# A hybrid decoder layer in float32: in the FFN-in units the form T2 is made by an accumulating DMA instead of a VectorE sum

## What is computed

```python
def swiglu_ffn(x, w_in, w_out):
    gate, up = jnp.split(x @ w_in, 2, axis=-1)      # w_in: 2048 x 11008
    return (jax.nn.silu(gate) * up) @ w_out

x = x + 0.5 * swiglu_ffn(rmsnorm(x, ffn1_norm), ffn1_w_in, ffn1_w_out)
...
x = x + mixed @ w_out
x = x + 0.5 * swiglu_ffn(rmsnorm(x, ffn2_norm), ffn2_w_in, ffn2_w_out)
```

## Time and profile before

| | |
|---|---|
| median of 3 runs | 1762.74 us |
| profiled execution: its time | 1762.94 us |
| profiled execution: its span | 1760.9 us |
| TensorE busy | 1753.6 us |
| VectorE busy | 1451.9 us |
| ScalarE busy | 1077.2 us |
| DMA: moved, mean rate | 371.29 MB, 211 GB/s |
| granted TensorE clock | 1.00 in every stretch looked at (2.4 GHz) |

### The profile page before, as it was taken

One profiled execution on the slowest core, in us unless ns is written; L12 is line 12 of the kernel. 1 busy time (PEld: TensorE's weight loads), 2 busy tenths in 40 slices (PEclk: granted clock), 3 DMA queues, 4 the chain that ended last, 5 costly groups with the idle time before them and its releaser, 6 DMA issues.

```text
span 1760.9 us, 20876 instructions
## 1 busy us (share of the span) xinstructions
PE 1753.6 (100%) x8036; PEld 1462.5 (83%) x8036; DVE 1451.9 (82%) x1607; ACT 1077.2 (61%) x1359; POOL 53.9 (3%) x54
## 2 busy tenths in 40 slices
PE   9999999999999999999999999999999999999999
PEld 7888888888988888888888888888888888988887
DVE  7988888888899998575655655888888888899998
ACT  7666666666666666454545544666666666666665
POOL 0000000000000001100000000000000000000000
PEclk9999999999999999999999999999999999999999
DMA  9877666676655556555455447576777776664762
GB/s 378 256 238 236 221 215 215 215 225 190 225 215 190 204 215 209 181 189 181 156 189 165 170 168 263 145 233 219 226 236 236 237 236 216 207 207 164 259 215 88
DMA packets 165490, 371.29 MB, mean 211 GB/s; under 512 B 6184, under 2 KB 15936, under 8 KB 165264
## 3 DMA queue, kind: packets, MB, share of 16 engines
q1 hardware_dynamic: 152288, 342.02, 54.9%
q0 software_dynamic: 11984, 25.98, 7.9%
q10 hardware_dynamic: 1120, 1.97, 0.3%
HBM read 367.82 MB, written 3.69 MB: 211 GB/s over the span
## 4 chain that ended last, share of the span: by engine, by line
PE 95%; DVE 2%; SPq 1%; DMA 1%; issue 0%; ACT 0%; ACTq 0%; DVEq 0%
PE bank L582 9%; PE bank L580 9%; PE bank L581 9%; PE bank L564 7%; PE bank L566 7%; PE bank L565 7%; PE bank L521 7%; PE bank L523 7%; PE bank L522 7%; PE bank L651 5%; PE bank L652 5%; PE bank L653 5%; PE bank L678 3%; PE bank L677 3%; PE bank L679 3%; PE bank L549 1%
## 5 line engine op out<-in xcount | busy, mean ns | idle before, releaser
L1185 DVE TENSOR_TENSOR wlo<-raw,whi 128x1024 fp32r<-128x1024 f32 (+1 forms) x586 | 698.3, 1207 | 215.4 <-ACT whi L847 207.7
L847 ACT ACTIVATE whi<-raw 128x1024 fp32r<-128x1024 f32 (+1 forms) x586 | 611.2, 1047 | 379.6 <-PE bank L523 189.3
L580 PE MATMUL bank<-whi,xs 128*128 128x512 f32 (+1 forms) x768 | 297.6, 388 | 1.7 <-DVE xs L1374 1.6
L582 PE MATMUL bank<-whi,xs 128*128 128x512 f32 (+1 forms) x768 | 295.5, 385 | 0.0
L581 PE MATMUL bank<-wlo,xs 128*128 128x512 f32 (+1 forms) x768 | 295.3, 385 | 0.0
L847 ACT ACTIVATE whi<-tsum 128x1024 fp32r<-128x1024 f32 (+1 forms) x120 | 122.4, 1037 | 110.4 <-PE bank L582 64.1
L580 PEld LDWEIGHTS bank<-whi,xs 128*128 128x128 f32 x768 | 144.2, 188 | 30.1 <-DVE wlo L1371 2.2
L582 PEld LDWEIGHTS bank<-whi,xs 128*128 128x128 f32 x768 | 144.1, 188 | 27.7
L581 PEld LDWEIGHTS bank<-wlo,xs 128*128 128x128 f32 x768 | 144.3, 188 | 26.8
L651 PE MATMUL bank<-whi,aw_hi 128*128 128x512 f32 x420 | 164.0, 390 | 0.0
L653 PE MATMUL bank<-whi,aw_lo 128*128 128x512 f32 x420 | 163.5, 389 | 0.0
(11 more groups left out here) (204 smaller groups left out, 2704.7 us busy)
## 6 DMA issues: line engine op xcount, KB each, us to landing
raw<-ffn_w_in SPq DMA_DIRECT2D x158, 1024.0 KB, 7.1
raw<-ffn_w_out SPq DMA_DIRECT2D x84, 1024.0 KB, 6.5
raw<-w_in SPq DMA_DIRECT2D x48, 1024.0 KB, 5.0
tsum<-ffn_w_in POOLq DMA_DIRECT2D x18, 1024.0 KB, 8.5
raw<-w_out SPq DMA_DIRECT2D x16, 1024.0 KB, 4.9
raw<-ffn_w_in SPq DMA_DIRECT2D x16, 768.0 KB, 5.5
x<-x SPq DMA_DIRECT2D x4, 512.0 KB, 12.4
raw<-ffn_w_out SPq DMA_DIRECT2D x4, 512.0 KB, 3.6
```

Of the source, the lines that this page charges most:

```text
L580: mm(banks[b][:, 0:w], xs[:, k + i, 0, tok], hi, start=starts[b] and k + i == 0, stop=False, skip_group_check=True)
L582: last = mm(banks[b][:, 0:w], xs[:, k + i, 1, tok], hi, start=False, stop=k + i == last_k, skip_group_check=True)
L847: A(whi[:, h % SLOTS, 0:n_el], src, ACT.Copy).then_inc(weights_hi, 1)
L1185: V.tensor_tensor(wlo[:, h % SLOTS, 0:n_el], src, whi[:, h % SLOTS, 0:n_el].bitcast(f32), ALU.subtract).then_inc(weights_lo, 1)
```

## The change

T2 is made like T4: when both halves of T1 are split, a DMA of the POOL queue adds B22 from device memory onto T1 in `tsum` (`add_piece(u, j, "B22", T1, t2_added)`). `sum_t2` is gone; VectorE keeps T1 and T3. ScalarE waits for `t2_added` before it copies T2, and for the sum of T3 before it copies T3. `free` now names B11's split as the last reader of B11's raw buffer. B22 is thus read from device memory twice, once by SP's queue into its raw buffer and once by POOL's onto `tsum`.

```diff
--- before.py
+++ after.py
@@ -321,8 +321,8 @@
         ga_hi, ga_ready, gs_summed, gs_hi, gs_ready, out_sums, p1_copied, p_joined = (
             sem(n) for n in ("ga_hi", "ga_ready", "gs_summed", "gs_hi", "gs_ready", "out_sums", "p1_copied", "p_joined"))
         xg_ready, s_summed, s_hi, s_ready = (sem(n) for n in ("xg_ready", "s_summed", "s_hi", "s_ready"))
-        sums_done, t4_added, copied, w_done, gate_added, c11_done = (
-            sem(n) for n in ("sums_done", "t4_added", "copied", "w_done", "gate_added", "c11_done"))
+        sums_done, t2_added, t4_added, copied, w_done, gate_added, c11_done = (
+            sem(n) for n in ("sums_done", "t2_added", "t4_added", "copied", "w_done", "gate_added", "c11_done"))
         sq_done, hss_ready, hms_ready, hr_ready, hsc_ready, qn_ready, qk_psum, qkT_ready, v_ready = (
             sem(n) for n in ("sq_done", "hss_ready", "hms_ready", "hr_ready", "hsc_ready", "qn_ready", "qk_psum", "qkT_ready", "v_ready"))
         f_psum, f_copied, f_added, f_z_ready, f_m_ready, f_exped, f_logged, nlf_ready = (
@@ -347,9 +347,7 @@
                         j, i = (n - IN_P[u]) // 8, (n - IN_P[u]) % 8
                         if j == 0:
                             return weights_lo, IN[u] + 2 * i + 2
-                        if i == LOAD["B11"]:
-                            return sums_done, 3 * ((UNITS - 1) * u + j)
-                        last = {LOAD["B21"]: B21, LOAD["B12"]: T3, LOAD["B22"]: B22, LOAD["G0"]: G0, LOAD["G1"]: G1, LOAD["U0"]: U0, LOAD["U1"]: U1}[i]
+                        last = {LOAD["B11"]: B11, LOAD["B21"]: B21, LOAD["B12"]: T3, LOAD["B22"]: B22, LOAD["G0"]: G0, LOAD["G1"]: G1, LOAD["U0"]: U0, LOAD["U1"]: U1}[i]
                         return weights_lo, unit_half(u, j) + last + 2
                     end = (QKV_P, END_P)[u]
                     if OUT_P[u] <= n < end:
@@ -470,15 +468,17 @@
             pool.wait_ge(vec_stored, 16)
             pool.dma_start(scratch, vec_dram.to_broadcast([P, H_A * VEC])).then_inc(vec_copied, 16)
 
-            def add_b21(u, j):
-                up = slice(D_FF + W * j, D_FF + W * j + UNIT_W[j])
-                pool.wait_ge(weights_lo, unit_half(u, j) + T2 + 2)
-                pool.dma_start(tsum[:, 0:4 * UNIT_W[j]].rearrange("p (k f) -> p k f", k=4),
-                               io[f"ffn{u + 1}_w_in"][0].rearrange("(k p) f -> p k f", p=P)[:, 12:16, up],
-                               accum_op=ALU.add).then_inc(t4_added, 16)
+            def add_piece(u, j, name, after, done):
+                n, w = IN_P[u] + 8 * j, UNIT_W[j]
+                k, col = {"B22": (12, W * j), "B21": (12, D_FF + W * j)}[name]
+                pool.wait_ge(weights_lo, unit_half(u, j) + after + 2)
+                pool.dma_start(tsum[:, 0:4 * w].rearrange("p (k f) -> p k f", k=4),
+                               io[f"ffn{u + 1}_w_in"][0].rearrange("(k p) f -> p k f", p=P)[:, k:k + 4, col:col + w],
+                               accum_op=ALU.add).then_inc(done, 16)
 
             for j in range(1, UNITS):
-                add_b21(0, j)
+                add_piece(0, j, "B22", T1, t2_added)
+                add_piece(0, j, "B21", T2, t4_added)
             pool.wait_ge(weights_lo, out_half(0, PASSES - 1, ("form", OUT_GROUPS[1] - 1, "T4")) + 1)
             pool.dma_start(wf[:], io["w_in"][0].rearrange("(k p) f -> p k f", p=P)[:, :, 6 * D_A:6 * D_A + H_B]).then_inc(f_loaded, 16)
             pool.dma_start(f_bias[:], io["forget_bias"].to_broadcast([P, H_B])).then_inc(f_loaded, 16)
@@ -505,7 +505,8 @@
                 pool.tensor_tensor(hr[:], hms[:], neg_half[:].rearrange("p (b i) -> p b i", b=TB), ALU.pow).then_inc(hr_ready, 1)
             x_power(2)
             for j in range(1, UNITS):
-                add_b21(1, j)
+                add_piece(1, j, "B22", T1, t2_added)
+                add_piece(1, j, "B21", T2, t4_added)
 
         @block.tensor
         def _(pe):
@@ -979,7 +980,7 @@
                 Y, V, Z, X = unit_banks(j)
                 base, n, w, s = unit_half(u, j), IN_P[u] + 8 * j, UNIT_W[j], j % 2
                 first, w2 = (UNITS - 1) * u + j - 1, 2 * w
-                act_e.wait_ge(sums_done, 3 * first + 1)
+                act_e.wait_ge(sums_done, 2 * first + 1)
                 for i in range(2):
                     split(base + T1 + i, tsum[:, i * w2:(i + 1) * w2], w2)
                 loaded(n + LOAD["B11"])
@@ -993,12 +994,13 @@
                 act_e.wait_ge(weights_used, base + B11 + 2)
                 act_e.wait_ge(act_f_done, 2 * (UNITS * u + j))
                 A(p1s[:, 0:w], Y[:, 0:w], ACT.Copy).then_inc(copied, 1)
-                act_e.wait_ge(sums_done, 3 * first + 3)
+                act_e.wait_ge(t2_added, 16 * (first + 1))
                 for i in range(2):
                     split(base + T2 + i, tsum[:, i * w2:(i + 1) * w2], w2)
                 loaded(n + LOAD["B21"])
                 for i in range(2):
                     split(base + B21 + i, piece_half(n + LOAD["B21"], i, w2), w2)
+                act_e.wait_ge(sums_done, 2 * first + 2)
                 split(base + T3, piece_half(n + LOAD["B12"], 0, w2), w2)
                 act_e.wait_ge(weights_used, base + T2 + 2)
                 A(gset[:, s, 0, 0:w], Y[:, 0:w], ACT.Copy).then_inc(copied, 1)
@@ -1350,15 +1352,8 @@
             def sum_t3(u, j):
                 n, w = IN_P[u] + 8 * j, UNIT_W[j]
                 full(n + LOAD["B22"])
-                dve.wait_ge(sums_done, 3 * ((UNITS - 1) * u + j - 1) + 1)
+                dve.wait_ge(sums_done, 2 * ((UNITS - 1) * u + j - 1) + 1)
                 V.tensor_tensor(whole(n + LOAD["B12"], w), whole(n + LOAD["B22"], w), whole(n + LOAD["B12"], w),
-                                ALU.add).then_inc(sums_done, 1)
-
-            def sum_t2(u, j):
-                n, w = IN_P[u] + 8 * j, UNIT_W[j]
-                dve.wait_ge(sums_done, 3 * ((UNITS - 1) * u + j - 1) + 2)
-                dve.wait_ge(weights_lo, unit_half(u, j) + B11 + 2)
-                V.tensor_tensor(tsum[:, 0:4 * w], whole(n + LOAD["B12"], w), whole(n + LOAD["B11"], w),
                                 ALU.add).then_inc(sums_done, 1)
 
             def plain_unit(u):
@@ -1403,7 +1398,6 @@
                 swiglu(u, j - 1)
                 split(base + B11 + 1, piece_half(n + LOAD["B11"], 1, w2), w2)
                 split(base + G0, piece_half(n + LOAD["G0"], 0, w2), w2)
-                sum_t2(u, j)
                 split(base + G0 + 1, piece_half(n + LOAD["G0"], 1, w2), w2)
                 for i in range(2):
                     split(base + T2 + i, tsum[:, i * w2:(i + 1) * w2], w2)
```

## The result

| | before | after |
|---|---|---|
| median of 7 runs each | 1763.09 us | 1768.71 us (1767.47 to 1769.38) |
| ratio to before | | 1.0032, 95% interval 1.0023 to 1.0042 |
| profiled execution: time, span | 1762.94, 1760.9 us | 1768.71, 1766.9 us |

The change makes the kernel 5.6 us slower, by 0.32%. The forecast was 1764.2 us with a range up to 1766.6 us, so it was wrong: right in the unit that is late, too small in how late the add comes there, and without the price of the clock that fell behind the wait.

The account below looks back on a forecast made before the run. TensorE's instruction count was taken as the bound. To the profiled 1762.94 us came 1.3 + 0.5 - 0.35 = 1.45 us in unit 1 of FFN 1, giving 1764.4 us, or 1764.2 us for the median; range 1762.4 to 1766.6 us.

Parts of the forecast that it names:

- TensorE's instructions set the time; VectorE's 44 us give nothing: Whole kernel: removing the T2 sum takes about 44 us off VectorE, none on TensorE's path; gain 0.
- Margin of 2.3 us in the later units: Wide units after the first: T2's first half is in hand 2.3 us before TensorE wants it; cost 0.
- Margins of 0.78 and 0.35 us in the two first units: Unit 1 of FFN 2 has 0.78 us of room before T2, unit 1 of FFN 1 0.35 us, if undisturbed.
- The copy puts the add back by 1.3 us: Unit 1 of FFN 1: `bias_vectors`, ahead in the POOL queue, delays the T2 add by 1.3 us, bounds 0 to 2.2.
- U0's load puts it back by 0.5 us: Unit 1 of FFN 1: SP's earlier U0 load delays the T2 add by 0.5 us, bounds 0 to 2.7 us.
- equal shares: Rival, first units: packets take turns with U0's load; 3.05 us, or 3.95 with the copy's 2.2; 6% over 3.5 us.
- What a wait costs: Unit 1 of FFN 1: TensorE cannot catch up, so its 1.45 us lateness is added in full.
- Late in every unit: Rival, T2's ScalarE copy: U0's load is served ahead of the add; 11.3 us in all, 1774 us; 4%.
- all hidden: Rival, unit 1 of FFN 1: the add slips between copy and U0, late under 0.7 us; 1762.5 to 1763.4 us; 25%.
- faster: Rival: VectorE is freed where TensorE waited for it; nothing to find over 3.5 us; 1%.
- First is served first: DMA queues, add against U0's load: the transfer there first is mostly served first, the basis for 0.5 us.
- Unit 1 of FFN 2: There U0's load delays the T2 add by 0.5 us, which the margin of 0.78 us takes; cost 0.

Follow-up runs that it names:

- e4: Changed kernel plus 30 identity transposes on TensorE ahead of T2 in unit 1 of FFN 1; 1766.58 us, ratio 1.0021.
- e8: Changed kernel with T2 by DMA in 19 units and by the old VectorE sum in unit 1 of FFN 1; 1762.90 us, ratio 1.0002.
- e5: Changed kernel with the large `bias_vectors` copy behind FFN 1's last add and U0's load waiting for T2's first split; 1763.38 us, ratio 1.0003.
- e3: Changed kernel with `bias_vectors` issued behind unit 1's two adds and U0's load waiting for T2's first split; 1766.30 us, ratio 1.0021.
- e2: Changed kernel with U0's load waiting for the split of T2's first half, the copy left ahead of the adds; 1764.63 us, ratio 1.0011.
- e6: Changed kernel with the large `bias_vectors` copy behind FFN 1's last add, U0's load left early; 1764.21 us, ratio 1.0008.
- e1: Changed kernel with the copy `bias_vectors` issued behind unit 1's two adds, U0's load left early; 1767.63 us, ratio 1.0027.
- e9: e5 with the T2 add held back in seven units so that TensorE waits before T2; 1798.65 us, ratio 1.0200.
- e10: e9 with identity transposes on TensorE in the seven waits; 1791.58 us, ratio 1.0161.

## Why the prediction was wrong, point by point

Two terms of the sum failed. The put-back of the add in unit 1 of FFN 1 was 1.3 + 0.5 = 1.8 us in it and measured 12.5 - 8.5 = 4.0 us. And the wait was taken at its own length, with nothing for the clock behind it, which measured 2.88 us. The second is what takes the time out of the range: without it the median would be some 1765.8 us (an estimate, 1768.71 - 2.88), and e4, which has the wait but not the fall, measured 1766.58 us, just inside.

- *TensorE's instructions set the time; VectorE's 44 us give nothing.* Right: 44.6 us off VectorE, unit 7 unchanged, e8 the same as before.
- *Margin of 2.3 us in the later units.* Right: 2.31 us in unit 7.
- *Margins of 0.78 and 0.35 us in the two first units.* Right as the room without a disturbance: e5 has no wait in either. The 0.35 us hold for an execution that starts like the profiled one of before. e3's does, and its margin is 0.36 us (T2's first half in hand at 64.32 us, TensorE there at 64.68 us). In the changed kernel's profiled execution T1 was split at 51.87 us and TensorE would have come at 63.96 us, 12.09 us, a margin of 0.94 us.
- *The copy puts the add back by 1.3 us.* Too small: 2.0 us (e2's 10.5 us against 8.5 us in e3), near the bound of 2.2 us. In the changed kernel the add comes to its full rate only from 57 us on (58 packets of its queue in the microsecond before, 96 and 99 in the two behind), when the copy's packets are through; that is some 4.8 us after its issue, in place of 3.9 us in e6.
- *U0's load puts it back by 0.5 us.* **This step failed**, in two ways. It was sized from the earlier trace rows, where a load was mostly served behind what was there first. Once it had begun, it shared packet for packet (197 to 183), as the rule of the "equal shares" rival has it. And it was sized apart from the queueing. A late add meets more of the load: 2.0 us (12.5 us against e2's 10.5 us), against 0.7 us when on time (e1, e6).
- *What a wait costs.* **This step failed too, as the term that was missing.** The sum took 1.45 us of waiting for 1.45 us of time. The wait was 3.25 us and its price 6.1 us, because TensorE ran at half clock behind it and took 2.88 us more. With the waits in the forecast's bounds (up to 4.55 us) this was to be foreseen as a possibility, and neither the sum nor a rival had it.
- *Rivals.* "Late in every unit", "all hidden" and "faster" did not come. "Equal shares in the first units" was the case at 6%, and its price of 3.05 to 3.95 us was again the wait without the clock. "First is served first" was a reading of the earlier trace rows alone.
- *Unit 1 of FFN 2.* Nearly right: 0.11 us before T2 and 0.12 us behind it, for a forecast of 0; the add landed after 9.2 us, 0.7 us late, for a forecast of 0.5 us.

The end of 4.55 us for one unit stood in the text, but the range ended at 1766.6 us.

## What to carry to other kernels

When work moves from an engine to a transfer, the average unit is not the one to check: look for the unit whose queue or whose neighbours differ, above all the first, and add up the disturbances in order of time, since one delay moves the transfer into the next. Where the bounding engine is TensorE, a wait of some microseconds is to be priced with what the clock can lose behind it (here 2.9 us behind a wait of 3.25 us, and 1.5 to 2.8 us in e9's five falls; nothing behind idle times of 1.66 and 2.09 us). If a wait can't be avoided, fill most of it with idle transposes, which kept the clock in e4 and e10; and taking 44 us off an engine that no one waits for is worth nothing.

## What the runs showed of the hardware that was not expected

- A load issued while an accumulating transfer is at work not only shares with it but lands late even where little is left of that transfer: U0's load took 10.4 us in unit 1, and 7.8 us in unit 7 (issued at 312.08 us), where it had taken 4.9 us. No one waits for it there.
- A load behind the copy within device memory is held back for long: e3's, issued 1.1 us after it, took 12.1 us in place of 5.0 us.
- The fall of the clock has no fixed price. In e9 five falls, with idle times of 2.79 to 5.00 us, left mean clocks of 0.53 to 0.77 in the six to seven microseconds behind them, in no order of the idle times, and cost 1.5 to 2.8 us. By which rule it fell behind 2.79 us and not behind 2.75 us stays open.
